# One dense block's expert sums kept in two PSUM banks over all 64 expert pairs, the other four blocks on two banks instead of four

## The chip, the core and the metric

The kernel runs on one core of a Trainium2 chip. The metric is the device time of one execution in microseconds (us), lower is better. Three runs before the change gave 3097.13, 3100.46 and 3105.5 us; the median is 3100.46 us. A core has five engines that run side by side and meet only at semaphores: TensorE (PE in the profile, PEld its weight load), VectorE (DVE), ScalarE (ACT), GpSimd (POOL) and SyncE (SP, which issues DMAs). PE writes only to PSUM, which here is used as eight banks of 128 partitions x 512 float32.

## The reference, cut to what matters

One transformer layer over 1024 tokens of width 1024: a mixer (pooling and windowed attention), then a layer of 16384 one-neuron experts, of which each of 8 heads picks 16 for each token.

```python
u = jnp.take(expert_down, eb, axis=0)
act = jax.nn.gelu(jnp.einsum('td,thkd->thk', hb, u))
wv = gb * act
vv = jnp.take(expert_up, eb, axis=0)
y = jnp.einsum('thk,thkd->td', wv, vv)
x = x + y
return rms_norm(x, g_final)
```

For one token this is the sum over its chosen experts of gate x gelu(h . down) x up. Summed over all 16384 experts with a gate of zero for those not chosen it is the same number, and that is the form the change touches.

## The kernel before, in words

Three stages follow one another: the mixer (and the choice of experts), a table of gates, and `experts`, which starts near 1240 us and ends the kernel. Only `experts` is changed.

The 1024 tokens are 8 blocks of 128. Three blocks (`DB`) are done *by rows*: POOL gathers the chosen experts' rows from HBM by indirect DMA (512 KB for 128 tokens), and DVE multiplies and adds them (L1517 for the down rows, L1529 for the up rows). There are 3 x 256 = 768 such row steps. Up to eight gathers (`RU`) are under way or unread at a time. The other five blocks (`ND`) are done *densely*: PE multiplies them with all 128 tiles of 128 experts. The tiles come in 64 pairs (`NPAIR`), and the loop over pairs `p` drives every engine; each pair also carries 12 of the row steps.

In pair `p`, PE alternates two kinds of work. `down_half(p + 1, q, half)` (L1381 to L1383, 24 matmuls) multiplies a half of the five blocks with a down tile of the *next* pair, into `abank` (two banks). Its two halves done, the semaphore `a_ready` lets ACT apply gelu (L1430), DVE multiply by the gates (`weights`, L1565), ACT make the rounded copy `w_hi` and DVE the rest `w_lo` (`weights_rest`, L1569). `up_product(p, t)` (L1397 to L1399, 12 matmuls in two groups of six) multiplies the weights of block `t` with both up tiles of pair `p`, into two banks of `ybank`, one for each half of the 1024 columns. The order of PE in a pair is written out: down, up 0, down, up 1, down, up 2, down, up 3, up 4. Each operand is split in a rounded high part and a low part, hence three matmuls per product.

After each up product DVE adds its two banks to the running sum `y` in SBUF (`add_y`, L1576, one instruction for each bank). A bank may be written again only when its last content has been added: PE waits on `y_added`. With four banks, product number `n` (over all pairs) waits for the adds of product `n - 2`.

Where DVE meets these adds is fixed by its own program. In pair `p`: `add_y(p - 1, 4)`; 3 row steps; `add_y(p, 0)`; 3 row steps; `weights(p + 1, 0)`; 1 row step; `add_y(p, 1)`; `weights_rest(p + 1, 0)`; 3 row steps; `add_y(p, 2)`; 2 row steps; `weights(p + 1, 1)`; `add_y(p, 3)`; `weights_rest(p + 1, 1)`. POOL's program in pair `p` is: 2 gathers, `down_rest` (L1336), 4 gathers, `up_rest` (L1340), 2 gathers, `down_rest`, 4 gathers, `up_rest`. `down_rest` makes the low part of a down tile and needs ACT's rounded copy of it (`down_high_of`, L1418), which ACT makes after the gelu of the same half pair.

After the loop DVE adds the last product, and the five blocks are normalised (L1498, L1545) and stored.

Of the kernel before, what the change touches and what calls it, by code (L numbers as in the profile page):

```python
# [6 lines left out]
P = 128  # L7
# [22 lines left out]
ND = NBLK - DB  # L30
# [9 lines left out]
F32 = mybir.dt.float32  # L40
# [3 lines left out]
ALU = mybir.AluOpType  # L44
# [1035 lines left out]
NPAIR = NK // 2  # L1080
# [119 lines left out]
def experts(nc, io, scr):  # L1200

    NOP = 8
    with ExitStack() as ctx:
# [3 lines left out]
        def sem(name):  # L1207
            return ctx.enter_context(nc.semaphore(name))
# [11 lines left out]
        tup_hi, tup_lo = sb("tup_hi", [P, 2, 2, D], F32R), sb("tup_lo", [P, 2, 2, D], F32R)  # L1220
        gates = sb("gates", [P, 2, NTC, 2, TC])
        w = sb("w", [P, 2, DT])
        w_hi, w_lo = sb("w_hi", [P, 2, 2, DT], F32R), sb("w_lo", [P, 2, 2, DT], F32R)
        y = sb("y", [P, ND, D])
        h2T = up[:, 0:KD * DT // D].rearrange("p a d -> p (a d)").rearrange("p (k n) -> p k n", k=KD)
        abank = ctx.enter_context(nc.psum_tensor("abank", [P, 2, 512], F32))
        ybank = [ctx.enter_context(nc.psum_tensor(f"ybank{i}", [P, 512], F32)) for i in range(4)]
        acc = ctx.enter_context(nc.psum_tensor("acc", [P, D], F32))
        h2_row = acc

# [21 lines left out]
        w_ready, w_high, w_low = sem("w_ready"), sem("w_high"), sem("w_low")  # L1252
        y_ready = sem("y_ready")
        y_added = sem("y_added")
        y_in = sem("y_in")

        block = ctx.enter_context(nc.Block())
# [111 lines left out]
        @block.tensor  # L1369
        def _(pe):  # L1370
            def down_half(p, q, half, first=False):
                if half == 0:
                    pe.wait_ge(down_low, 2 * p + q + 1)
                    if 2 * p + q:
                        pe.wait_ge(gl_ready, 2 * p + q)
                out, ts = abank[:, half, 0:HT], slice(half * HT, (half + 1) * HT)
                for k in range(KD):
                    if first:
                        pe.wait_ge(h2T_low, k + 1)
                    at = slice(k * P, (k + 1) * P)  # L1380
                    nc.tensor.matmul(out, tdown_hi[:, q, at], h2T_hi[:, k, ts], start=k == 0, stop=False)  # L1381
                    nc.tensor.matmul(out, tdown_hi[:, q, at], h2T_lo[:, k, ts], start=False, stop=False)  # L1382
                    ins = nc.tensor.matmul(out, tdown_lo[:, q, at], h2T_hi[:, k, ts], start=False, stop=k == KD - 1)  # L1383
                if half == 1:
                    ins.then_inc(a_ready, 1)

            def up_product(p, t):
                if t == 0:
                    pe.wait_ge(w_low, 2 * (p + 1))
                    pe.wait_ge(up_low, 2 * (p + 1))  # L1390
                r, n, ts = p % 2, ND * p + t, slice(t * P, (t + 1) * P)
                for i in range(2):
                    if n >= 2:
                        pe.wait_ge(y_added, 2 * (n - 2) + i + 1)
                    out, ds = ybank[n % 2 * 2 + i][:], slice(i * 512, (i + 1) * 512)
                    for q in range(2):
                        nc.tensor.matmul(out, w_hi[:, r, q, ts], tup_hi[:, r, q, ds], start=q == 0, stop=False)  # L1397
                        nc.tensor.matmul(out, w_hi[:, r, q, ts], tup_lo[:, r, q, ds], start=False, stop=False)  # L1398
                        ins = nc.tensor.matmul(out, w_lo[:, r, q, ts], tup_hi[:, r, q, ds], start=False, stop=q == 1)  # L1399
                    ins.then_inc(y_ready, 1)  # L1400

            for q in range(2):
                for half in range(2):
                    down_half(0, q, half, first=q + half == 0)
            for p in range(NPAIR):
                for t in range(ND):
                    if p + 1 < NPAIR and t < 4:
                        down_half(p + 1, t // 2, t % 2)
                    up_product(p, t)

        @block.scalar
        def _(act):
            def down_high_of(p, q):

                act.wait_ge(tdown_in[q], 16 * (p + 1))
                if p:
                    act.wait_ge(a_ready, 2 * (p - 1) + q + 1)
                nc.scalar.activation(tdown_hi[:, q], tdown[:, q], ACT.Copy).then_inc(down_high, 1)  # L1418

            def up_high_of(p, q):  # L1420
                act.wait_ge(tup_in[q], 16 * (p + 1))
                if p >= 2:
                    act.wait_ge(y_ready, 2 * ND * (p - 1))
                nc.scalar.activation(tup_hi[:, p % 2, q], tup[:, q], ACT.Copy).then_inc(up_high, 1)  # L1424

            def expert_gelu(p, q):
                act.wait_ge(a_ready, 2 * p + q + 1)
                if p:
                    act.wait_ge(w_low, 2 * (p - 1) + q + 1)
                nc.scalar.activation(w[:, q].rearrange("p (h n) -> p h n", h=2), abank[:, :, 0:HT],  # L1430
                                     ACT.Gelu_apprx_tanh).then_inc(gl_ready, 1)

            def weights_high(p, q):
                act.wait_ge(w_ready, 2 * p + q + 1)
                if p >= 2:
                    act.wait_ge(y_ready, 2 * ND * (p - 1))
                nc.scalar.activation(w_hi[:, p % 2, q], w[:, q], ACT.Copy).then_inc(w_high, 1)

            def keep_h2(b):
                act.wait_ge(h2_in, 16 * (b + 1))  # L1440
                if b:
                    act.wait_ge(acc_read, b)
                nc.scalar.activation(h2_row[:], h2[:], ACT.Copy).then_inc(h2_kept, 1)

            def root(c, n):
                act.wait_ge(var_ready, c + 1)
                nc.scalar.activation(stat[:, 2, 0:n], stat[:, 1, 0:n], ACT.Sqrt).then_inc(std_ready, 1)

            def row_events(rows):

                for n in rows:
                    kind, b, k = ROWS[n]
                    if kind == "dot" and k == NSEL - 1:
                        act.wait_ge(row_used, n + 1)
                        nc.scalar.activation(act_of[:, b], act_of[:, b], ACT.Gelu_apprx_tanh).then_inc(dots_act, 1)
                    if kind == "up" and k == NSEL - 1:
                        if b + 1 < DB:
                            keep_h2(b + 1)
                        root(b, 1)

            down_high_of(0, 0)
            act.wait_ge(h2T_in, 32)
            for k in range(KD):
                nc.scalar.activation(h2T_hi[:, k], h2T[:, k], ACT.Copy).then_inc(h2T_halved, 1)
            down_high_of(0, 1)
            for q in range(2):
                up_high_of(0, q)
            for q in range(2):
                expert_gelu(0, q)
                down_high_of(1, q)  # L1470
            for q in range(2):
                weights_high(0, q)
            keep_h2(0)
            for p in range(NPAIR):
                a, b = parts(rows_of_pair(p), (5, 5))
                if p + 1 < NPAIR:
                    up_high_of(p + 1, 0)
                row_events(a)
                if p + 1 < NPAIR:
                    expert_gelu(p + 1, 0)  # L1480
                if p + 2 < NPAIR:
                    down_high_of(p + 2, 0)
                if p + 1 < NPAIR:
                    up_high_of(p + 1, 1)
                    weights_high(p + 1, 0)
                row_events(b)
                if p + 1 < NPAIR:
                    expert_gelu(p + 1, 1)
                if p + 2 < NPAIR:
                    down_high_of(p + 2, 1)  # L1490
                if p + 1 < NPAIR:
                    weights_high(p + 1, 1)
            act.wait_ge(normed, DB)
            for t in range(ND):
                act.wait_ge(y_added, 2 * (ND * (NPAIR - 1) + t + 1))
                if t == 0:
                    act.wait_ge(row_used, NROW)
                nc.scalar.activation(up[:, t], y[:, t], ACT.Square, accum_out=stat[:, 0, t:t + 1]).then_inc(ssq_ready, 1)  # L1498
            root(DB, ND)

        @block.vector
        def _(dve):
# [66 lines left out]
                nc.vector.tensor_tensor(w_lo[:, p % 2, q], w[:, q], w_hi[:, p % 2, q].bitcast(F32), ALU.subtract).then_inc(w_low, 1)  # L1569

            def add_y(p, t):
                n = ND * p + t
                for i in range(2):
                    dve.wait_ge(y_ready, 2 * n + i + 1)
                    part = y[:, t, i * 512:(i + 1) * 512]
                    nc.vector.tensor_tensor(part, part, ybank[n % 2 * 2 + i][:], ALU.add).then_inc(y_added, 1)  # L1576

            for k in range(KD):
                dve.wait_ge(h2T_halved, k + 1)
# [7 lines left out]
            for p in range(NPAIR):  # L1587
                more = p + 1 < NPAIR
                a, b, c, d, e = parts(rows_of_pair(p), (3, 2, 1, 3, 1))
                if p:  # L1590
                    add_y(p - 1, ND - 1)
                for n in a:
                    row(n)
                add_y(p, 0)
# [111 lines left out]
```

## Time and profile before

| | us |
|---|---|
| median of three runs | 3100.46 |
| the profiled execution | 3103.28 |
| its span | 3101.5 |
| `experts`, about | 1240 to 3101.5 |
| the 61 pairs from 1321.2 to 3035 | 1713.8 |

| engine | busy over the span | in 1321.2 to 3035 |
|---|---|---|
| PE | 2827.1 us (91%) | 1699.4 us (99%) |
| DVE | 2338.5 us (75%) | 1525.4 us (89%) |
| POOL | 2130.4 us (69%) | 1355.7 us (79%) |
| ACT | 929.9 us (30%) | 416.2 us (24%) |

The second column is the sum over two windows of the trace. A busy PE is one that has a matmul in its pipeline; consecutive matmuls overlap, so the durations of single ones (0.31 and 0.39 us) are longer than the distance between their starts (0.14 and 0.23 us). A row "[0.79 <-DMA up<-in_down,e_idx]" in a timeline says that the engine stood idle for 0.79 us before this instruction and that the landing of that DMA ended it. "x2" behind a row is two like instructions merged into one row, whose duration is then from the start of the first to the end of the second.

### The profile page before, as it was taken

To read this page: it belongs to the slowest core of one execution; us is meant where nothing else is said; L and a number is where in the kernel's file an instruction comes from. 1 tells how busy PE (TensorE), PEld (TensorE's weight loads), DVE (VectorE), ACT (ScalarE), POOL (GpSimd) and SP (SyncE) were. 2 spreads that over 40 slices of the span, in tenths; PEclk is the share of its full clock that TensorE was granted. 3 is DMA by queue.
4 is the path that set the end of the run, shared out by engine and by line. 5 is a ranking of instruction groups with operands and counts; after the bars stand their busy time and mean duration, and the time that the engine had idled before them with its cause. 6 is when DMAs were issued, how large, how long until landed. Compare 5 with 4: busy or idle time off the path is not lost.

```text
span 3101.5 us, 40038 instructions
## 1 busy us (share of the span) xinstructions
PE 2827.1 (91%) x15235; PEld 2473.4 (80%) x15235; DVE 2338.5 (75%) x4356; ACT 929.9 (30%) x1230; POOL 2130.4 (69%) x1553
## 2 busy tenths in 40 slices
PE   7999889998791598699999999999999999999996
PEld 6688777676681487599989998999999989999985
DVE  2322497335399698488898888898898888899888
ACT  4232433222430498222222222222222222222221
POOL 4334576246576697577887877788777877788774
PEclk9899999899895799799999999999999999999998
DMA  4122421022310378988999998989988889998886
GB/s 143 35 68 96 163 69 63 33 68 75 135 56 0 86 225 237 331 323 328 328 327 326 328 330 301 328 327 329 326 328 326 330 300 329 327 330 321 327 318 223
DMA packets 268048, 716.48 MB, mean 231 GB/s; under 512 B 20496, under 2 KB 106256, under 8 KB 267728
## 3 DMA queue, kind: packets, MB, share of 16 engines
q0 software_dynamic: 111152, 404.54, 34.9%
q1 hardware_dynamic: 156704, 309.38, 30.2%
q8 instruction: 121, 1.98, 0.2%
q14 instruction: 71, 0.58, 0.1%
HBM read 657.47 MB, written 56.36 MB: 230 GB/s over the span
## 4 chain that ended last, share of the span: by engine, by line
PE 48%; DVE 4%; POOL 3%; DMA 3%; issue 1%; ACT 1%; DVEq 0%; SPq 0%; ACTq 0%
PE abank L1383 8%; PE abank L1381 8%; PE abank L1382 8%; PE ybank L1397 8%; PE ybank L1398 8%; PE ybank L1399 8%; DVE acc L1529 2%; DMA up<-in_up,e_idx 2%; POOL up L1331 2%; POOL tdown_lo L1336 1%; DVE y L1576 1%; POOL tup_lo L1340 0%; DVE up L1517 0%; DMA up<-in_down,e_idx 0%; DMA e_h<-all_h 0%
## 5 line engine op out<-in xcount | busy, mean ns | idle before, releaser
L1381 PE MATMUL abank<-h2T_hi,tdown_hi 128*128 128x320 f32 x2048 | 634.3, 310 | 38.8 <-DVE h2T_lo L1580 30.8
L1383 PE MATMUL abank<-h2T_hi,tdown_lo 128*128 128x320 f32 x2048 | 634.7, 310 | 0.0
L1382 PE MATMUL abank<-h2T_lo,tdown_hi 128*128 128x320 f32 x2048 | 634.4, 310 | 0.0
L1529 DVE SCALAR_TENSOR_TENSOR acc<-up,e_act,acc 128x1024 f32<-128x1024 f32 x381 | 489.5, 1285 | 87.1 <-DMA up<-in_up,e_idx 70.8
L728 POOL TENSOR_TENSOR m_wlo<-m_raw,m_whi 128x1024 fp32r<-128x1024 f32 x116 | 279.5, 2416 | 381.0 <-ACT m_whi L554 378.7
L1517 DVE CUSTOM_DVE_ANT_0 up<-up,acc 128x1024 f32<-128x1024 f32 x384 | 458.9, 1214 | 104.4 <-DMA up<-in_down,e_idx 94.3
L1397 PE MATMUL ybank<-tup_hi,w_hi 128*128 128x512 f32 x1280 | 504.3, 394 | 18.3 <-DVE y L1576 16.6
L1398 PE MATMUL ybank<-tup_lo,w_hi 128*128 128x512 f32 x1280 | 503.5, 393 | 0.0
L1399 PE MATMUL ybank<-tup_hi,w_lo 128*128 128x512 f32 x1280 | 500.4, 391 | 0.0
L1331 POOL DMA_INDIRECT up<-in_down,e_idx x384 | 406.0, 1057 | 98.2 <-issue 86.3
L1331 POOL DMA_INDIRECT up<-in_up,e_idx x384 | 399.2, 1040 | 103.4 <-issue 88.9
L1336 POOL TENSOR_TENSOR tdown_lo<-tdown,tdown_hi 128x1024 fp32r<-128x1024 f32 x128 | 308.6, 2411 | 204.0 <-ACT tdown_hi L1418 202.5
L1381 PEld LDWEIGHTS abank<-h2T_hi,tdown_hi 128*128 128x128 f32 x2048 | 386.6, 189 | 50.0 <-issue 40.2
L1576 DVE TENSOR_TENSOR y<-y,ybank 128x512 f32<-128x512 f32 x640 | 407.9, 677 | 0.7 <-PE ybank L1399 0.7
L1382 PEld LDWEIGHTS abank<-h2T_lo,tdown_hi 128*128 128x128 f32 x2048 | 386.5, 189 | 9.8
L1383 PEld LDWEIGHTS abank<-h2T_hi,tdown_lo 128*128 128x128 f32 x2048 | 386.2, 189 | 0.0
L1430 ACT ACTIVATE w<-abank 128x640 f32<-128x640 f32 x128 | 90.2, 705 | 904.5 <-PE abank L1383 904.5
L1340 POOL TENSOR_TENSOR tup_lo<-tup,tup_hi 128x1024 fp32r<-128x1024 f32 x128 | 309.4, 2417 | 9.4 <-ACT tup_hi L1424 7.2
L1397 PEld LDWEIGHTS ybank<-tup_hi,w_hi 128*128 128x128 f32 x1280 | 241.7, 189 | 65.8 <-DVE y L1576 19.9
L1399 PEld LDWEIGHTS ybank<-tup_hi,w_lo 128*128 128x128 f32 x1280 | 241.8, 189 | 52.7
L389 PE MATMUL bank<-m_hT,m_whi 128*128 128x512 f32 x656 | 264.3, 403 | 15.1 <-POOL m_wlo L728 12.1
L1398 PEld LDWEIGHTS ybank<-tup_lo,w_hi 128*128 128x128 f32 x1280 | 241.9, 189 | 40.8
(220 smaller groups left out, 4636.0 us busy)
## 6 DMA issues: line engine op xcount, KB each, us to landing
tdown<-in_downT SPq DMA_DIRECT2D x128, 512.0 KB, 6.5
tup<-in_up SPq DMA_DIRECT2D x128, 512.0 KB, 6.5
m_raw<-in_tiles SPq DMA_DIRECT2D x116, 512.0 KB, 3.3
all_table<-t_out SPq DMA_DIRECT2D x10, 4096.0 KB, 16.3
gates<-all_table SPq DMA_DIRECT2D x64, 640.0 KB, 5.0
up<-in_down,e_idx POOLq DMA_INDIRECT x384, 6.5
up<-in_up,e_idx POOLq DMA_INDIRECT x384, 6.7
m_x<-in_x SPq DMA_DIRECT2D x8, 512.0 KB, 5.8
```

The source lines that it names most:

```text
L1331: nc.gpsimd.indirect_dma_start(up[:, n % RU], None, io["up" if kind == "up" else "down"], bass.IndirectOffsetOnAxis(idx[:, b, k:k + 1], 0) ...
L1336: nc.gpsimd.tensor_tensor(tdown_lo[:, q], tdown[:, q], tdown_hi[:, q].bitcast(F32), ALU.subtract).then_inc(down_low, 1)
L1340: nc.gpsimd.tensor_tensor(tup_lo[:, p % 2, q], tup[:, q], tup_hi[:, p % 2, q].bitcast(F32), ALU.subtract).then_inc(up_low, 1)
L1381: nc.tensor.matmul(out, tdown_hi[:, q, at], h2T_hi[:, k, ts], start=k == 0, stop=False)
L1382: nc.tensor.matmul(out, tdown_hi[:, q, at], h2T_lo[:, k, ts], start=False, stop=False)
L1383: ins = nc.tensor.matmul(out, tdown_lo[:, q, at], h2T_hi[:, k, ts], start=False, stop=k == KD - 1)
L1397: nc.tensor.matmul(out, w_hi[:, r, q, ts], tup_hi[:, r, q, ds], start=q == 0, stop=False)
L1398: nc.tensor.matmul(out, w_hi[:, r, q, ts], tup_lo[:, r, q, ds], start=False, stop=False)
L1399: ins = nc.tensor.matmul(out, w_lo[:, r, q, ts], tup_hi[:, r, q, ds], start=False, stop=q == 1)
L1517: nc.vector.tensor_tensor_reduce(out=src, in0=src, in1=h2_row[:], scale=1.0, scalar=0.0, op0=ALU.mult, op1=ALU.add, accum_out=act_of[:, b, ...
L1529: nc.vector.scalar_tensor_tensor(out=acc[:], in0=src, scalar=act_of[:, b, k:k + 1], in1=acc[:], op0=ALU.mult, op1=ALU.add).then_inc(row_us ...
L1576: nc.vector.tensor_tensor(part, part, ybank[n % 2 * 2 + i][:], ALU.add).then_inc(y_added, 1)
```

## The change

`ybank` shrinks from four banks to two. The two banks gained become `ykept`, and the products of the last dense block (`t == 4`) of all 64 pairs accumulate in them: the start flag is set at pair 0 alone and the stop flag at pair 63. DVE adds `ykept` to `y` once, after the loop, so `add_y(p - 1, 4)` is gone from the loop. The products of blocks 0 to 3 share two banks, so that each waits for the adds of the product *just before it* among these four, and block 4 waits for no add. A new semaphore `pair_done` counts the products of block 4 and takes the place of `y_ready` where ACT waits for a whole pair to be done before it overwrites `tup_hi` or `w_hi`.

```diff
-        ybank = [ctx.enter_context(nc.psum_tensor(f"ybank{i}", [P, 512], F32)) for i in range(4)]
+        ybank = [ctx.enter_context(nc.psum_tensor(f"ybank{i}", [P, 512], F32)) for i in range(2)]
+        ykept = [ctx.enter_context(nc.psum_tensor(f"ykept{i}", [P, 512], F32)) for i in range(2)]
...
-                r, n, ts = p % 2, ND * p + t, slice(t * P, (t + 1) * P)
+                r, n, ts = p % 2, (ND - 1) * p + t, slice(t * P, (t + 1) * P)
+                kept = t == ND - 1
                 for i in range(2):
-                    if n >= 2:
-                        pe.wait_ge(y_added, 2 * (n - 2) + i + 1)
-                    out, ds = ybank[n % 2 * 2 + i][:], slice(i * 512, (i + 1) * 512)
+                    if not kept and n >= 1:
+                        pe.wait_ge(y_added, 2 * (n - 1) + i + 1)
+                    out, ds = (ykept if kept else ybank)[i][:], slice(i * 512, (i + 1) * 512)
                     for q in range(2):
-                        nc.tensor.matmul(out, w_hi[:, r, q, ts], tup_hi[:, r, q, ds], start=q == 0, stop=False)
+                        first, last = (p + q == 0, p + 1 == NPAIR and q == 1) if kept else (q == 0, q == 1)
+                        nc.tensor.matmul(out, w_hi[:, r, q, ts], tup_hi[:, r, q, ds], start=first, stop=False)
...
-                    ins.then_inc(y_ready, 1)
+                    ins.then_inc(pair_done if kept else y_ready, 1)
...
-                    act.wait_ge(y_ready, 2 * ND * (p - 1))
+                    act.wait_ge(pair_done, 2 * (p - 1))
...
-                act.wait_ge(y_added, 2 * (ND * (NPAIR - 1) + t + 1))
+                act.wait_ge(y_added, 2 * ((ND - 1) * (NPAIR - 1) + t + 1))
...
-                    dve.wait_ge(y_ready, 2 * n + i + 1)
+                    if kept:
+                        dve.wait_ge(pair_done, 2 * p + i + 1)
+                    else:
+                        dve.wait_ge(y_ready, 2 * n + i + 1)
...
-                if p:
-                    add_y(p - 1, ND - 1)
                 for n in a:
                     row(n)
```

No engine's other instructions move. On DVE at the end of a pair and the start of the next one, before the change (L1565 is `weights`, L1576 an add, L1569 `weights_rest`, L1517 a row step):

```order
L1565 TENSOR_TENSOR w<-w,gates 128x640 [waits gl_ready]
L1576 TENSOR_TENSOR y<-y,ybank0 128x512 [waits y_ready]
L1576 TENSOR_TENSOR y<-y,ybank1 128x512 [waits y_ready]
L1569 TENSOR_TENSOR w_lo<-w,w_hi 128x640 [waits w_high]
L1576 TENSOR_TENSOR y<-y,ybank2 128x512 [waits y_ready]
L1576 TENSOR_TENSOR y<-y,ybank3 128x512 [waits y_ready]
L1517 ISA up,e_act<-up,acc 128x1024 [waits up_in0]
```

and the same place of the changed kernel, whose lines are up to ten higher (L1571, L1586, L1575, L1523):

```order
L1571 TENSOR_TENSOR w<-w,gates 128x640 [waits gl_ready]
L1586 TENSOR_TENSOR y<-y,ybank0 128x512 [waits y_ready]
L1586 TENSOR_TENSOR y<-y,ybank1 128x512 [waits y_ready]
L1575 TENSOR_TENSOR w_lo<-w,w_hi 128x640 [waits w_high]
L1523 ISA up,e_act<-up,acc 128x1024 [waits up_in0]
```

The two adds of block 4 are gone; the first row step of the next pair follows `weights_rest` at once. On PE, at the end of the up product of one block and the start of `down_half` behind it nothing moves; what changes is the bank that each product writes, and so the add it waits for. The first matmul into each bank of the products of blocks 2, 3 and 4 in one pair, before:

```order
L1397 MATMUL ybank0<-tup_hi,w_hi 128x512 [waits y_added]
...
L1397 MATMUL ybank1<-tup_hi,w_hi 128x512 [waits y_added]
...
L1397 MATMUL ybank2<-tup_hi,w_hi 128x512 [waits y_added]
...
L1397 MATMUL ybank3<-tup_hi,w_hi 128x512 [waits y_added]
...
L1397 MATMUL ybank0<-tup_hi,w_hi 128x512 [waits y_added]
...
L1397 MATMUL ybank1<-tup_hi,w_hi 128x512 [waits y_added]
```

and after (L1403 is the line that was L1397):

```order
L1403 MATMUL ybank0<-tup_hi,w_hi 128x512 [waits y_added]
...
L1403 MATMUL ybank1<-tup_hi,w_hi 128x512 [waits y_added]
...
L1403 MATMUL ybank0<-tup_hi,w_hi 128x512 [waits y_added]
...
L1403 MATMUL ybank1<-tup_hi,w_hi 128x512 [waits y_added]
...
L1403 MATMUL ykept0<-tup_hi,w_hi 128x512
...
L1403 MATMUL ykept1<-tup_hi,w_hi 128x512
```

Products 1, 2 and 3 now write the bank that the product just before them wrote, and the one of block 4 waits for nothing on DVE.

## Rows read from the trace of the kernel before

**Rows 1.** Two windows: length; PE, PEld, DVE, ACT, POOL busy; clock; DMA share; GB/s.

```profile
1321.20:2024.70 703.50, 697.17 (x3902) 635.56 (x3901) 624.42 (x832) 171.40 (x205) 555.97 (x399) 1.00 0.89 324
2024.70:3035.00 1010.30, 1002.26 (x5616) 912.75 (x5615) 900.97 (x1149) 244.80 (x294) 799.71 (x576) 1.00 0.90 324
```

**Rows 2.** Waits over the span: who for whom, us, times, longest.

```profile
POOL tdown_lo L1336 <- ACT tdown_hi L1418: 202.5, 68, 23.3
DVE up L1517 <- DMA up<-in_down,e_idx: 94.3, 95, 3.9
DVE acc L1529 <- DMA up<-in_up,e_idx: 70.8, 79, 2.1
PE ybank L1397 <- DVE y L1576: 16.6, 7, 6.2
```

**Rows 3.** Timeline of PE, pair 26: products 0, 2, 3, next 0.

```profile
2024.72 0.39 PE L1397 MATMUL ybank<-tup_hi,w_hi 128*128 128x512 f32 x1
...
2030.84 0.31 PE L1383 MATMUL abank<-h2T_hi,tdown_lo 128*128 128x320 f32 x1
...
2037.24 0.39 PE L1397 MATMUL ybank<-tup_hi,w_hi 128*128 128x512 f32 x1
...
2043.50 0.39 PE L1397 MATMUL ybank<-tup_hi,w_hi 128*128 128x512 f32 x1
...
2052.48 0.39 PE L1397 MATMUL ybank<-tup_hi,w_hi 128*128 128x512 f32 x1
```

**Rows 4.** Timeline of DVE, pair 26, from before add 1 to add 2.

```profile
2033.24 2.77 DVE L1565 TENSOR_TENSOR w<-w,gates 128x640 f32<-128x640 f32 x1
...
2037.07 1.27 DVE L1576 TENSOR_TENSOR y<-y,ybank 128x512 f32<-128x512 f32 x2
...
2041.01 1.22 DVE L1517 CUSTOM_DVE_ANT_0 up<-up,acc 128x1024 f32<-128x1024 f32 x1 [0.79 <-DMA up<-in_down,e_idx]
...
2042.55 1.22 DVE L1517 CUSTOM_DVE_ANT_0 up<-up,acc 128x1024 f32<-128x1024 f32 x1 [0.32 <-DMA up<-in_down,e_idx]
...
2043.70 0.68 DVE L1576 TENSOR_TENSOR y<-y,ybank 128x512 f32<-128x512 f32 x1
```

**Rows 5.** Timelines of ACT and POOL, pair 26, after the second down half.

```profile
2031.18 0.71 ACT L1430 ACTIVATE w<-abank 128x640 f32<-128x640 f32 x1 [8.15 <-PE abank L1383]
...
2032.91 2.41 POOL L1336 TENSOR_TENSOR tdown_lo<-tdown,tdown_hi 128x1024 fp32r<-128x1024 f32 x1 [2.27 <-ACT tdown_hi L1418]
2035.48 1.36 POOL L1331 DMA_INDIRECT up<-in_down,e_idx  x1 [0.16 <-issue]
```

**Rows 6.** Timelines in pair 42: product 3, add 2, product 4.

```profile
2488.42 0.39 PE L1397 MATMUL ybank<-tup_hi,w_hi 128*128 128x512 f32 x1
...
2496.83 1.28 DVE L1576 TENSOR_TENSOR y<-y,ybank 128x512 f32<-128x512 f32 x2
...
2497.57 0.80 PE L1397 MATMUL ybank<-tup_hi,w_hi 128*128 128x512 f32 x1 [6.24 <-DVE y L1576]
```

**Rows 7.** Timelines, pairs 1 and 61: product 3 and add 2.

```profile
1339.97 0.39 PE L1397 MATMUL ybank<-tup_hi,w_hi 128*128 128x512 f32 x1
1340.74 1.28 DVE L1576 TENSOR_TENSOR y<-y,ybank 128x512 f32<-128x512 f32 x2
...
3026.37 0.39 PE L1397 MATMUL ybank<-tup_hi,w_hi 128*128 128x512 f32 x1
...
3026.63 1.28 DVE L1576 TENSOR_TENSOR y<-y,ybank 128x512 f32<-128x512 f32 x2
```

**Rows 8.** PE windows (busy, clock, DMA) after waits of pairs 10, 42.

```profile
1593.40:1603.00 9.60, 9.59 (x52) 1.00 0.87 284
2498.00:2506.00 8.00, 8.00 (x36) 0.74 0.77 236
```

**Rows 9.** Timeline of PE in pair 10: product 4.

```profile
1593.41 0.50 PE L1397 MATMUL ybank<-tup_hi,w_hi 128*128 128x512 f32 x1 [0.69 <-DVE y L1576]
```

**Rows 10.** L1565 over the span: duration ns min/median/max.

```profile
L1565 DVE TENSOR_TENSOR w<-w,gates x128: 815/1342/2765, 1272.3 to 3056.6; 128x640 f32<-128x640 f32 x128
```

More of the change, by code:

```diff
@@ L1254, in experts @@
         y_added = sem("y_added")
+        pair_done = sem("pair_done")
         y_in = sem("y_in")
@@ L1390, in up_product @@
                     pe.wait_ge(up_low, 2 * (p + 1))
-                r, n, ts = p % 2, ND * p + t, slice(t * P, (t + 1) * P)
+                r, n, ts = p % 2, (ND - 1) * p + t, slice(t * P, (t + 1) * P)
+                kept = t == ND - 1
                 for i in range(2):
-                    if n >= 2:
-                        pe.wait_ge(y_added, 2 * (n - 2) + i + 1)
-                    out, ds = ybank[n % 2 * 2 + i][:], slice(i * 512, (i + 1) * 512)
+                    if not kept and n >= 1:
+                        pe.wait_ge(y_added, 2 * (n - 1) + i + 1)
+                    out, ds = (ykept if kept else ybank)[i][:], slice(i * 512, (i + 1) * 512)
                     for q in range(2):
-                        nc.tensor.matmul(out, w_hi[:, r, q, ts], tup_hi[:, r, q, ds], start=q == 0, stop=False)
+                        first, last = (p + q == 0, p + 1 == NPAIR and q == 1) if kept else (q == 0, q == 1)
+                        nc.tensor.matmul(out, w_hi[:, r, q, ts], tup_hi[:, r, q, ds], start=first, stop=False)
                         nc.tensor.matmul(out, w_hi[:, r, q, ts], tup_lo[:, r, q, ds], start=False, stop=False)
-                        ins = nc.tensor.matmul(out, w_lo[:, r, q, ts], tup_hi[:, r, q, ds], start=False, stop=q == 1)
-                    ins.then_inc(y_ready, 1)
+                        ins = nc.tensor.matmul(out, w_lo[:, r, q, ts], tup_hi[:, r, q, ds], start=False, stop=last)
+                    ins.then_inc(pair_done if kept else y_ready, 1)
             for q in range(2):
@@ L1435, in weights_high @@
                 if p >= 2:
-                    act.wait_ge(y_ready, 2 * ND * (p - 1))
+                    act.wait_ge(pair_done, 2 * (p - 1))
                 nc.scalar.activation(w_hi[:, p % 2, q], w[:, q], ACT.Copy).then_inc(w_high, 1)
@@ L1571, in add_y @@
             def add_y(p, t):
-                n = ND * p + t
+                n = (ND - 1) * p + t
+                kept = t == ND - 1
                 for i in range(2):
-                    dve.wait_ge(y_ready, 2 * n + i + 1)
+                    if kept:
+                        dve.wait_ge(pair_done, 2 * p + i + 1)
+                    else:
+                        dve.wait_ge(y_ready, 2 * n + i + 1)
                     part = y[:, t, i * 512:(i + 1) * 512]
-                    nc.vector.tensor_tensor(part, part, ybank[n % 2 * 2 + i][:], ALU.add).then_inc(y_added, 1)
+                    nc.vector.tensor_tensor(part, part, (ykept if kept else ybank)[i][:], ALU.add).then_inc(y_added, 1)
             for k in range(KD):
```

## The prediction

> **What bounds the kernel now.** I read the busy shares by window first. In the steady loop, 1713.8 us for 61 pairs, PE is busy for 1699.4, so it stands idle for 14.4 us in all; DVE is at 89%, POOL at 79%, and the clock at its higher level (2.4 GHz, shown as 1.00) [rows 1]. PE is the bound, and DVE time that is saved is worth something only where PE waits for DVE. The waits of PE on an add come to 16.6 us in 7 places [rows 2]. A pair takes 2052.48 - 2024.72 = 27.76 us [rows 3], and 58 of the 63 pairs keep that time to 0.1 us or so but for pair 21, which is 8.5 us longer.
>
> The question is then how near the adds run behind the products. In pair 26, product 2 starts at 2037.24 [rows 3], and the first add of product 1 starts at 2037.07 and takes 0.68, so ends at 2037.75 [rows 4]. Product 3 starts at 2043.50 [rows 3], the first add of product 2 ends at 2043.70 + 0.68 = 2044.38 [rows 4]. With four banks neither matters. With two, both products would have had to wait.
>
> **Part 1: the two adds of block 4 that go.** 63 pairs x 2 adds, each 0.64 us (two take 1.28 [rows 7]) and paced at about 0.60, are 76 to 81 us of DVE. Nearly all of it is hidden: PE has 14.4 us of idle time to give back at most. I count it at nothing in the steady pairs, since DVE's next step is held by something else: it waits 94.3 + 70.8 = 165.1 us for gathers [rows 2], 2.6 us a pair. 1.2 us sooner at the start of a pair becomes 1.2 us more of that wait at the third row step. At the end of the kernel, where no tile parts are left to make and DVE runs row steps without a pause, one pair of adds (1.2 us) does come off the time.
>
> **Part 2: the bank wait.** What is late next is the add before each product, by how much depends on what sets the add's time. I followed add 2 of pair 26 back. Before it stand two row steps that waited for their gathers, 0.79 and 0.32 us [rows 4]. The gather for the first of them was issued at 2035.48, right behind `tdown_lo`, which started at 2032.91 when ACT's rounded copy came; that came behind the gelu at 2031.18, for which ACT had waited 8.15 us on PE [rows 5]: PE's last matmul of the second down half, at 2030.84 [rows 3]. So the time of add 2 hangs on PE's own work of the same pair, 2044.38 - 2030.84 = 13.54 us behind it, through ACT, POOL and a DMA of about 5.5 us (2041.01 - 2035.48). Neither the removed adds nor a PE that waits at product 2 or 3 changes that distance. A wait at product 3 therefore comes again in every pair and moves the whole pair behind it; it is not a delay that is paid once.
>
> Add 1 hangs on the same event: `weights` at 2033.24 takes 2.77 us instead of 0.815 [rows 4, 10], running beside `tdown_lo` and ending 0.7 us after it (2032.91 + 2.41 [rows 5]; 2036.01), then one row step, then the add. Product 2 would start 2037.75 - 2037.24 + 0.06 = 0.57 us late. The 0.06 is what a release costs: in pair 42 the first add ends at 2496.83 + 0.68 = 2497.51 and the waiting matmul starts at 2497.57 [rows 6]. Product 3 starts late by 2044.38 - 2043.50 + 0.06 = 0.94 us. The two are not added: product 3's start is fixed by add 2, whether product 2 was late or not, so the larger counts.
>
> I took this difference in every pair from 1 to 63. The first is 1340.74 + 0.68 - 1339.97 = 1.45 and pair 61 3026.63 + 0.68 - 3026.37 = 0.94 [rows 7]. Five pairs (10, 32, 42, 59, 63) are apart; over the other 58 the larger of the two differences has a mean of 1.16 (1.17 with the negative one of pair 62 set to nothing), and only that one of the 58 is below zero. Products 0 and 1 are safe in nearly all: 2.8 and 1.0 us of room. The second bank of each product has 0.7 to 0.8 us more room than the first.
>
> 58 x (1.16 + 0.06) = 70.8 us.
>
> The pairs apart: in pair 42 DVE finishes a row block and is 9 us late with add 2. PE got past product 3 at 2488.42 and waited 6.24 us at product 4, until 2497.57 [rows 6]. Now product 3 waits until then, and product 4, one product of 12 matmuls (2.75 us: 12 x 0.23), comes after. So this pair costs one product more, about 2.7 us. Pair 10 is the same with a small wait (0.69, at 1593.41 [rows 9]); for 32 and 59 I take the same: 4 x 2.7 = 10.8. Pair 63 has no down halves, PE waits there in any case and DVE's row block ends later than all products: nothing. Pair 0: product 1 would wait 6 us, but the next pair then waited for the weights anyway; I take 1.
>
> Sum: 70.8 + 10.8 + 1 - 1.2 = 81.4. With a pair of 29.0 us the DMA share of 0.90 [rows 1] falls to about 0.86, and gathers may land a little sooner; I take 0.05 us a pair off, -3. That leaves +78. The profiled execution took 3103.3 against a median of 3100.5, so from the median: 3100.5 + 78.4 = 3179.
>
> **Bounds.** Least: if gathers land so early that DVE no longer waits before add 2, it comes 0.79 + 0.32 = 1.11 us sooner and product 3 has room; what is left is product 2's wait, on which no gather bears. 58 x 0.6 (the median of that difference, 0.55, and the 0.06) = 35, and 10 for the pairs apart: 3145. Most: add 2 later than now by one `weights` (below), 58 x 0.8 = 46 more: 3225.
>
> **ACT's waits** on `pair_done` come true at the same matmul as before (the end of product 4), two pairs back; they cost nothing. The final adds are in the place they had.
>
> **Rivals.**
>
> *Only product 2 waits.* As under the least bound: 3145. For it: DMA is the busiest thing beside PE, and a slower pair relieves it. Against: the wait before add 2 would have to shrink by all of 1.1 us, for 4% less traffic.
>
> *The lock turns round.* `weights` and `tdown_lo` run one after the other today, `tdown_lo` first [rows 4, 5]. With DVE 1.2 us ahead, `weights` may start in the gap between the gelu's end (2031.18 + 0.71 = 2031.89) and 2032.91 [rows 5], and then POOL waits for 0.8 us [rows 10]; the gathers behind it and add 2 come as much later. Time: 3179 + 58 x 0.8 = 3225. The page "SBUF — State Buffer" of the Trainium skill (section "Who interferes with whom") says that a DVE instruction with two SBUF inputs contends with a GpSimd one that reads SBUF, and that issue order decides who blocks. The 2.77 us against 0.815 [rows 4, 10] agree with the first half. Against this rival: the step before `weights` is also held by gathers, so the 1.2 us are mostly gone by then.
>
> *Waits too short to see.* If all of DVE's steps move forward by the 1.2 us saved, add 1 and add 2 end before their products want the banks (0.57 and 0.94 are below 1.2), only the four pairs apart pay, and the time is 3100.5 + 10 - 3 = 3107, inside what counts as no change: a measurement of this kernel can tell 0.3%, 9 us, from none. Against: the waits for gathers named in part 2.
>
> *Faster.* One mechanism: PE's present waits on DVE, 14.4 us in all, go with DVE's load, at the pairs where DVE is late from a finished row block. It decides if the adds there run ahead by more than a product (2.75 us), so that the two-bank rule never binds. Time: 3100.5 - 14.4 - 1.2 = 3085. Against: in pair 42 DVE is 9 us late.
>
> *The clock.* PE now pauses once or twice in each pair. After the wait of 6.24 us of pair 42 the granted clock was 0.74 over 8 us, so for half of that at the lower level (1.2 GHz); after the 0.69 us of pair 10 it was 1.00 over 9.6 us [rows 8, 9]. If a wait of about 1 us cost like the long one, 2 us of work lost each time, the time would be 3179 + 62 x 2 = 3303. The page "TensorE: Matmul & The Clock Gate" of the Trainium skill (section "A second HAM failure mode: psum-queue depth-cycling") speaks for it: a PE that pauses briefly between groups of matmuls while it cycles through PSUM banks can swing between its two clocks. By this trace's short wait it does not.
>
> **Chances.** Forecast 0.63 (its own range 3163 to 3198: 0.95 to 1.5 us a pair), only product 2 waits 0.12, lock 0.11, clock 0.04: slower by over 0.3% together 0.90. Waits too short to see 0.06: same. Faster 0.04. The range takes in the two neighbours up to their bounds, 3142 to 3216.
>
> **What the profile after would show.** DVE's line of adds with 514 instead of 640 instructions. PE idle before the first matmul of product 3 (L1403), released by DVE's add, about 60 times and about 1.2 us each, some 0.6 of it already at product 2; PE's busy share in the loop at 95 or 96%; a pair of 29.0 us; DVE's waits for gathers longer by about 2.4 us a pair (the 1.2 saved and the 1.2 of the longer pair); the granted clock still 1.00. It would be wrong if PE's idle time at L1403 is below 0.3 us a pair, if the distance from the second down half's end to add 2 is not about 13.5 us, or if the clock falls.

## The result, and the profile after

The changed kernel takes 3173.57 us (median of six runs, 3168.19 to 3185.41) against 3100.49 us: a ratio of 1.0238, 95% interval 1.0213 to 1.0262. It is slower by 73 us; 78 us had been forecast. The profiled execution took 3168.92 us with a span of 3167.1, 65.6 us over the span before. Its mean granted clock is 0.957, before it was 0.955.

The windows over the same loop, in the columns of [rows 1]:

```profile
1320.00:2050.00 730.00, 704.38 (x3886) 633.04 (x3885) 604.36 (x783) 172.98 (x205) 551.58 (x400) 1.00 0.86 312
2050.00:3099.00 1049.00, 1013.85 (x5601) 910.75 (x5600) 866.98 (x1073) 246.04 (x294) 795.45 (x574) 1.00 0.86 311
```

PE is busy for 1718.2 of 1779 us, 96.6% where it was 99.2%; the DMA share fell from 0.90 to 0.86, and the clock stayed at 1.00. The waits, in the columns of [rows 2]:

```profile
POOL tdown_lo L1340 <- ACT tdown_hi L1424: 274.8, 100, 23.1
DVE up L1523 <- DMA up<-in_down,e_idx: 161.7, 111, 4.1
DVE acc L1535 <- DMA up<-in_up,e_idx: 115.5, 91, 4.0
PE ybank L1403 <- DVE y L1586: 66.0, 87, 8.3
```

PE's waits on an add went from 7 with 16.6 us to 87 with 66.0 us. DVE's waits for gathers rose by 112 us, 1.8 us a pair. This is DVE's row of the costliest groups (add instructions, busy time, mean, idle before it):

```profile
L1586 DVE TENSOR_TENSOR y<-y,ybank 128x512 f32<-128x512 f32 x512 | 327.8, 678 | 11.4 <-PE ybank L1405 11.3
```

With the two adds of `ykept` at the end there are 514 instead of 640. The 126 adds took some 79 us of DVE with them (the row before has 407.9 us for 640), and the time rose.

Over the pairs 1 to 61, product 3 waits in 60 and product 2 in 37. One pair shows both waits. PE in pair 22 (the starts of product 0, of the last matmul of the second down half, of products 1, 2, 3 with its second matmul, and of the next product 0), which answers to [rows 3]:

```profile
1934.37 0.39 PE L1403 MATMUL ybank<-tup_hi,w_hi 128*128 128x512 f32 x1
...
1940.48 0.31 PE L1387 MATMUL abank<-h2T_hi,tdown_lo 128*128 128x320 f32 x1
1940.63 0.39 PE L1403 MATMUL ybank<-tup_hi,w_hi 128*128 128x512 f32 x1
...
1947.45 0.50 PE L1403 MATMUL ybank<-tup_hi,w_hi 128*128 128x512 f32 x1 [0.40 <-DVE y L1586]
...
1954.07 0.50 PE L1403 MATMUL ybank<-tup_hi,w_hi 128*128 128x512 f32 x1
1954.41 0.40 PE L1404 MATMUL ybank<-tup_lo,w_hi 128*128 128x512 f32 x1
...
1963.15 0.39 PE L1403 MATMUL ybank<-tup_hi,w_hi 128*128 128x512 f32 x1
```

and DVE in it, which answers to [rows 4]:

```profile
1943.64 2.01 DVE L1571 TENSOR_TENSOR w<-w,gates 128x640 f32<-128x640 f32 x1
...
1946.72 1.27 DVE L1586 TENSOR_TENSOR y<-y,ybank 128x512 f32<-128x512 f32 x2
...
1950.93 1.22 DVE L1523 CUSTOM_DVE_ANT_0 up<-up,acc 128x1024 f32<-128x1024 f32 x1 [1.06 <-DMA up<-in_down,e_idx]
...
1953.34 1.28 DVE L1586 TENSOR_TENSOR y<-y,ybank 128x512 f32<-128x512 f32 x2
```

The first add of product 1 ends at 1946.72 + 0.68 = 1947.40 and product 2 starts at 1947.45; the first add of product 2 ends at 1954.02 and product 3 starts at 1954.07. The steps between products are 6.82 and 6.62 us where they were 6.26, and the pair takes 28.78 us. The timelines of ACT and POOL, against [rows 5]:

```profile
1940.83 0.71 ACT L1436 ACTIVATE w<-abank 128x640 f32<-128x640 f32 x1 [8.65 <-PE abank L1387]
...
1942.56 2.41 POOL L1340 TENSOR_TENSOR tdown_lo<-tdown,tdown_hi 128x1024 fp32r<-128x1024 f32 x1 [3.25 <-ACT tdown_hi L1424]
1945.12 1.36 POOL L1335 DMA_INDIRECT up<-in_down,e_idx  x1
```

From PE's last matmul of the second down half to the end of the first add of product 2 it is 1954.02 - 1940.48 = 13.54 us, as in pair 26 before (that the second decimal agrees is chance; the medians are below). The chain that ended last tells the same: PE had 48% of the span in it and now has 22%, DMA 14% (3% before), DVE 10% (4%), POOL 7% (3%).

### The profile page after: what moved, and what is told of

Same layout as the page of the kernel before. It is cut to its first block, busy times and chain, and to the rows that moved or that the text cites. A ratio compares the mean times of both kernels' runs of the same rounds, so it can differ in the third digit from the quotient of the medians.

```text
span 3167.1 us, 39912 instructions
## 1 busy us (share of the span) xinstructions
PE 2850.9 (90%) x15235; PEld 2473.3 (78%) x15235; DVE 2285.4 (72%) x4230; ACT 934.0 (29%) x1230; POOL 2126.1 (67%) x1553
## 4 chain that ended last, share of the span: by engine, by line
PE 22%; DMA 14%; DVE 10%; POOL 7%; issue 5%; ACT 2%; DVEq 0%; SPq 0%; ACTq 0%
DMA up<-in_up,e_idx 7%; DMA up<-in_down,e_idx 6%; POOL tdown_lo L1340 4%; DVE acc L1535 4%; PE abank L1387 4%; PE abank L1385 4%; PE abank L1386 4%; PE ybank L1403 3%; PE ybank L1404 3%; PE ybank L1405 3%; POOL up L1335 3%; DVE up L1523 2%; ACT tdown_hi L1424 2%; DVE y L1586 2%; DVE w L1571 1%
## 5 line engine op out<-in xcount | busy, mean ns | idle before, releaser
L1523 DVE CUSTOM_DVE_ANT_0 up<-up,acc 128x1024 f32<-128x1024 f32 x384 | 459.5, 1216 | 169.6 <-DMA up<-in_down,e_idx 161.7
L1403 PE MATMUL ybank<-tup_hi,w_hi 128*128 128x512 f32 x1024 | 414.3, 405 | 68.2 <-DVE y L1586 66.0
L1335 POOL DMA_INDIRECT up<-in_down,e_idx x384 | 393.2, 1024 | 97.7 <-issue 83.0
L1404 PE MATMUL ybank<-tup_lo,w_hi 128*128 128x512 f32 x1024 | 403.7, 394 | 0.0
L1405 PE MATMUL ybank<-tup_hi,w_lo 128*128 128x512 f32 x1024 | 401.7, 392 | 0.0
L1586 DVE TENSOR_TENSOR y<-y,ybank 128x512 f32<-128x512 f32 x512 | 327.8, 678 | 11.4 <-PE ybank L1405 11.3
L1403 PEld LDWEIGHTS ybank<-tup_hi,w_hi 128*128 128x128 f32 x1024 | 193.8, 189 | 128.3 <-DVE y L1586 92.7
L391 PE MATMUL bank<-m_hT,m_wlo 128*128 128x512 f32 x656 | 257.9, 393 | 0.0
L390 PE MATMUL bank<-m_hlo,m_whi 128*128 128x512 f32 x656 | 257.2, 392 | 0.0
```

What stands on the lines that cost most here:

```text
L1335: nc.gpsimd.indirect_dma_start(up[:, n % RU], None, io["up" if kind == "up" else "down"], bass.IndirectOffsetOnAxis(idx[:, b, k:k + 1], 0) ...
L1523: nc.vector.tensor_tensor_reduce(out=src, in0=src, in1=h2_row[:], scale=1.0, scalar=0.0, op0=ALU.mult, op1=ALU.add, accum_out=act_of[:, b, ...
L1586: nc.vector.tensor_tensor(part, part, (ykept if kept else ybank)[i][:], ALU.add).then_inc(y_added, 1)
```

## The experiments

Below, *distance* is the time from the modelled end of that last down matmul (about 0.3 us after its start) to the end of the first add of product 2, as the median over the pairs 1 to 61: 13.60 us before, 13.36 us in the changed kernel. *Pair* is the median time of a pair: 27.76 and 28.93. All are edits of the changed kernel unless said otherwise. Each ratio is against runs of the kernel before made beside that experiment, whose medians are 3099.05, 3100.0 or 3103.2 us, so it can differ a little from the quotient with 3100.49.

**Both adds early.** DVE's order alone.

```diff
-                a, b, c, d, e = parts(rows_of_pair(p), (3, 2, 1, 3, 1))
+                a, b, c, d, e = parts(rows_of_pair(p), (3, 3, 1, 1, 4))
...
+                add_y(p, 1)
                 if more:
                     weights(p + 1, 0)
                 for n in c:
                     row(n)
-                add_y(p, 1)
```

> The changed kernel with DVE's order alone altered: the add of block 1 goes ahead of `weights(p+1, 0)` and one row step, the add of block 2 ahead of the two row steps that wait for their gathers (it stands behind one row step and not three). If the loss is the bank wait and nothing else, the first add of product 1 ends near 10 us into the pair and that of product 2 near 16.2, both before the 12.5 and 18.8 at which PE wants the banks: PE's wait for DVE falls under 15 us, a pair is back at 27.8 us, and the time is 3100 us (3090 to 3108). If the loss lay in the accumulation over 64 pairs itself, in the clock, or in DVE and POOL blocking each other in another order, the time stays near 3170.

Measured: 3103.86 us, ratio 1.0009 (1.0001 to 1.0018). Pair 27.76. Nothing but the place of two adds was altered, and 70 of the 73 us are back; accumulation over 64 pairs costs nothing that shows in a steady pair. PE's waits on adds did not fall under the 15 us expected; this is what is left of them (who waited for whom, us, times, longest):

```profile
PE ybank L1403 <- DVE y L1586: 18.1, 5, 6.9
```

**Add 1 early alone** (the second half of that edit, with the shares left as they were).

> The changed kernel with only the add of block 1 moved ahead of `weights(p+1, 0)` and one row step. If the waits of one pair are not added, because product 3 starts when add 2 is done whether product 2 was late or not, then product 2's wait of 0.6 us goes and product 3's grows to the full 1.2: 3173 us (3167 to 3180). If they are added, 0.6 us x 61 = 35 us come back: 3138.

Measured: 3198.4 us, ratio 1.031 (1.0292 to 1.0329). Product 2 no longer waits (6.26 us from product 1), and nothing came back, so the waits do not add, as expected. But it is 25 us slower still, which neither side had. The distance grew to 13.78 us and the pair to 29.33. PE waits once a pair (97.0 us in 65 places).

The 0.4 us more of distance come at row step 9 (steps are numbered from 0 within a pair). Step 8 starts where it did, 10.0 us behind the down half. Step 9 starts at 11.94 and not 11.49, though its gather is issued at 5.99 us in both kernels: it lands 5.89 us after its issue and not 5.48 (all medians). Why it lands later is not settled.

**Add 2 early alone** (the shares of the first edit, add 1 where it was).

> The changed kernel with only the add of block 2 moved, to stand before the two row steps that wait for their gathers. Product 3's wait goes and product 2's stays at 0.6 us: a pair of 28.4 us, 3173 - 61 x 0.6 = 3137 us (3128 to 3147). If the two waits had one cause apart from the place of the add (a slower DVE, the clock), the time stays near 3173.

Measured: 3140.89 us, ratio 1.0139 (1.0125 to 1.0154). Pair 28.45, which is 0.69 over 27.76, with all of it at product 2 (6.86 us from product 1, so a wait of 0.60); product 3 starts 6.37 us after it. As expected, but for the last 0.1 us: product 3 itself does not wait, and 6.37 is 0.11 over 6.26. That is what PE loses behind a wait, beside the wait (below, under the sum). PE's waits on adds are 44.5 us in 63 places.

**Two gathers early.** POOL's order alone: row steps 8 and 9 are gathered ahead of `tdown_lo`.

```diff
-                a, b, c, d = parts(rows_of_pair(p), (2, 3, 2, 3))
+                a, b, c, d = parts(rows_of_pair(p), (2, 4, 4, 2))
```

> The changed kernel with POOL's order alone altered: two gathers of the last part of a pair (row steps 8 and 9) go ahead of the `tdown_lo` that waits for ACT, two stay behind it. My account says that add 2 hangs on that chain: PE's second down half, gelu, rounded copy, `tdown_lo`, gather. Then row steps 8 and 9 find their rows there, add 2 comes about 1 us sooner, product 3's wait beyond product 2's goes: 3140 us (3130 to 3155). If add 2 is late for another reason (DVE's own load, the DMA engines' traffic), the time stays within 8 us of 3173, or rises because `tdown_lo` starts later.

Measured: 3133.09 us, ratio 1.0108 (1.0092 to 1.0125). The distance fell to 10.33 us. No instruction of DVE or PE was touched, and 40 us are back: the adds were late through the gathers behind `tdown_lo`.

The time is in the range expected, but by another mix of pairs than the one expected, and so by luck. Add 2 came 3.0 us sooner, not 1. Product 2's wait did not stay in every pair: of the pairs 1 to 61, 42 take 27.8 us and wait for no add. In 45 pairs `weights` had run ahead of `tdown_lo`, and add 1 was in time. Another 18 take over 29 us, most of them 30.2. In 17 of these 18 (not in pair 42, where DVE finishes a row block), and in no other pair, the first `w_lo` of the pair takes over 1.5 us. Pair 26, DVE and then POOL:

```profile
2049.10 3.45 DVE L1575 TENSOR_TENSOR w_lo<-w,w_hi 128x640 fp32r<-128x640 f32 x1
...
2055.89 1.27 DVE L1586 TENSOR_TENSOR y<-y,ybank 128x512 f32<-128x512 f32 x2
```

```profile
2049.45 2.40 POOL L1344 TENSOR_TENSOR tup_lo<-tup,tup_hi 128x1024 fp32r<-128x1024 f32 x1
```

`w_lo`, 0.82 us at the median, takes 3.45 us and ends 0.7 us after `tup_lo`: the same picture as `weights` beside `tdown_lo` in [rows 4, 5]. This pair has the longest `w_lo`; in the others `tup_lo` starts some 0.2 us ahead of `w_lo`, which then takes 2.9 us.

**One gather early** (shares 2, 4, 3, 3), to test that reading.

> The changed kernel with one gather (row step 8) moved ahead of `tdown_lo`, three behind it, where an earlier experiment moved two. There, the POOL subtraction `tup_lo` came 6.9 us behind PE's second down half, just before DVE's `w_lo` at about 7.1, and 26 `w_lo` took over 1.5 us and not 0.8 (3 in the changed kernel); its pairs took 27.8 or 30.2 us. With three gathers behind it `tup_lo` starts near 8.2, after `w_lo`. If DVE and POOL blocked each other there, the 30.2 us pairs go and no more than some five `w_lo` are long; row step 9 still starts about 1.5 us sooner than in the changed kernel, so that product 3 waits little beyond product 2: 3133 us (3120 to 3148). If the 30.2 us pairs have another cause, they stay.

Measured: 3139.19 us, ratio 1.0109 (1.0092 to 1.0126). Pair 28.45: the pairs of 27.8 and 30.2 us are gone but for single ones. `tup_lo` came 8.8 us behind the down half. Product 2's 0.6 us is what is left. The time was hit. `w_lo` took over 1.5 us 15 times, not 26 and not the expected five, but 13 of the 15 are the second `w_lo` of a pair, beside a `tdown_lo`, and these pairs take 28.4 or 28.8 us but for the pairs 0 and 21, which are long in every kernel. At the place that made the slow pairs, the first `w_lo` beside `tup_lo`, no pair from 1 to 61 has a long one. That the two blocked each other there is borne out; that the blocking moved to the second `w_lo` was not expected.

**The bank rule alone.** Block 4 gets its two banks but starts afresh in each pair, and DVE adds it in each pair.

```diff
-                        first, last = (p + q == 0, p + 1 == NPAIR and q == 1) if kept else (q == 0, q == 1)
+                        first, last = q == 0, q == 1
...
+                if p:
+                    add_y(p - 1, ND - 1)
```

(and a semaphore of its own for these adds, on which the next product of block 4 waits.)

> The bank rule without the removed adds: blocks 0 to 3 share two banks, block 4 has its own two, but its products start afresh in each pair and DVE adds them in each pair, as in the kernel before. If the 126 adds are worth nothing in the steady loop, as I counted them, the time is that of the changed kernel, plus 1 to 2 us at the end: 3175 us (3168 to 3182). If DVE's relief had hidden part of the loss, up to 1.2 us a pair, the time is up to 3245.

Measured: 3182.54 us, ratio 1.026 (1.0244 to 1.0275). Pair 28.99, distance 13.44. All of the loss is there without the removed adds. The time lies 0.5 us above the range expected. Beside 1.0238 (1.0213 to 1.0262) of the changed kernel it is 9 us more, but the intervals overlap; the median pair accounts for 0.06 x 61 = 4 us of them.

**The removed adds alone.** The kernel before with four banks; 63 of the 64 sums of block 4 are made and never added.

> The removed adds without the bank rule: the kernel before with its four banks, in which the products of block 4 are made in every pair but added only after the last one (so the sums of block 4 lack 63 of 64 pairs). By my account 1.2 us comes off the end and a few us at the places where DVE is late from a finished row block: 3096 us (3088 to 3100.5). If PE's present waits on DVE all go with the load: 3086. If DVE had been a bound in the steady loop, 27.8 us a pair would fall, and the time with it by tens of us.

Measured: 3098.64 us, ratio 0.9995 (0.9985 to 1.0005). Pair 27.76. 126 adds of DVE are worth nothing that can be measured. In the trace the idle time of DVE before the third row step of a pair grew from 1.19 to 2.11 us (means over the pairs 1 to 61), which is where the prediction said the 1.2 us would go.

**The kernel before, reordered** (four banks, all adds, the order of DVE of the first experiment).

> The kernel before (four banks, all adds) with the order of DVE that the first experiment has: add 1 ahead of `weights(p+1, 0)`, add 2 ahead of the last four row steps. With four banks PE waits for the adds only at the finished row blocks, so the order should be worth little: 3098 us (3092 to 3102). Beside the first experiment it tells what two kept banks are worth once their wait is gone: by my account the 1.2 us at the end and a few us at the row blocks.

Measured: 3094.0 us, ratio 0.998 (0.997 to 0.9991). It is the fastest of all, and beats both kernels.

```profile
PE ybank L1397 <- DVE y L1576: 3.3, 3, 2.1
```

Against the first experiment, with 18.1 us of waits on adds, this is what four banks give where DVE is late, in pair 0 (6.9 of the 18.1 us) and at the finished row blocks: 10 us in the medians, 15 us in the waits. The trace of this kernel is of its fastest execution (3088.46 us), so the 15 says too much. The two kept banks lose to the two spare ones even when no steady pair waits. I had expected the opposite sign.

**Add 2 late.** One more row step ahead of it (the shares are 3, 3, 1, 4, 1).

> The changed kernel with the add of block 2 one row step later (behind rows 7 to 10 of a pair, not 7 to 9). In the changed kernel the add's first half ends 13.36 us behind PE's second down half and a pair takes 28.93; a row step is 1.2 to 1.3 us. If product 3's wait is the whole cause, the distance grows to 14.6 and the pair by the same 1.25 us, one for one: 3173.6 + 61 x 1.25 = 3250 us (3238 to 3262). If part of the delay is caught up elsewhere (DMA relief, other waits), the time rises by less than 60 us.

Measured: 3354.36 us, ratio 1.0797 (1.0773 to 1.082), 181 us over the changed kernel (173 by the two ratios). The expectation of 76 failed, and on the side that I had not named. The distance grew by 2.0 us, to 15.35, and the pair by 3.42, to 32.35. Of the 2.0, 0.57 is row step 9, which starts at 12.06 us behind the down half and not at 11.49, as in the second experiment and as little settled; the rest is the row step added and its wait. The wait of pair 24, and windows over the pairs 24 and 25, the 9.5 us up to the wait's end and the 9.3 us from there on (length, PE busy, clock, DMA share, GB/s):

```profile
2080.76 0.50 PE L1403 MATMUL ybank<-tup_hi,w_hi 128*128 128x512 f32 x1 [3.15 <-DVE y L1586]
```

```profile
2058.67:2125.24 66.57, 60.52 (x314) 0.92 0.77 282
2071.20:2080.70 9.50, 6.42 (x38) 1.00 0.92 329
2080.70:2090.00 9.30, 9.24 (x39) 0.82 0.90 327
```

With waits of some 3 us the clock goes to its lower level (1.2 GHz) for a part of the work: 0.82 in the 9.3 us after this one. The mean granted clock of the execution is 0.934 against 0.957. In the pairs 1 to 61 the trace's record of the clock has 44 stretches at the lower level, 178 us in all, where the changed kernel has 3 and 17 us.

The two parts can be told apart. The distance grew by 1.84 us at the mean, 61 x 1.84 = 112 of the 183 us that these 61 pairs took longer. The other 71 are the clock: in 43 pairs it was low around the start of product 3, and from there to product 4 it took 4.44 us where it was 2.85, 43 x 1.59 = 68. The other 18 pairs waited nearly as long with the clock at its higher level, and there pair time less distance is 15.57 us, the number of the other kernels below.

## Why the prediction was right

*What bounds the kernel.* PE did, as read from the windows, and time saved on DVE was worth nothing: the removed adds alone gave 0.9995 (0.9985 to 1.0005). Of PE's 14.4 us of idle time none came back that can be measured.

*The chain behind add 2.* It was right in all its links, and it is shown, not only argued: moving the add back by its place in DVE's order took the wait at product 3 away, and so did, in 42 of 61 pairs, the place of two gathers in POOL's order, each without the other. With the end of the down half as the starting point, pair time and distance differ by the same number in the three kernels whose pairs wait at product 3: 28.93 - 13.36 = 15.57, 29.33 - 13.78 = 15.55, 28.99 - 13.44 = 15.55. To these come the 18 pairs of the last experiment with 15.57. This difference is PE's own work from product 3 to the next down half; what was forecast is that the distance does not shrink when PE gets later, and it did not, but for 0.2 us. That is the "comes again in every pair" of the prediction. For the kernel before this sum would give 13.60 + 15.56 = 29.16; it took 27.76, since its four banks did not ask for the add.

*The sum.* The 61 pairs from 1 to 61 took 1784.7 us against 1714.2: +70.5. The pairs 10, 32, 42 and 59 gave +4.27, +1.72, +2.44 and +0.02, together 8.5 (forecast 10.8), and pair 21, which I had among the steady ones, -1.4. The other 56 gave +1.13 us each at the mean, 63.5 together (+1.17 at the median; forecast 1.22, less 0.05). The end from pair 62 on is 1.2 us shorter, as forecast. Pair 0 is 1.2 us shorter where I had +1, and the stage began 2.5 us sooner in this execution, which is no effect of the change. 70.5 - 1.2 - 1.2 - 2.5 = 65.6, as the spans have it. Pair 62, which the prediction counts among those that keep 27.76 us, takes 24.2 us in both kernels.

*Two terms of it were too small, and they cancel.* That the steady pair came out so close is in part luck. In means over the 56 pairs, the steps are:

| | forecast | measured |
|---|---|---|
| add 2 ends after product 3 wants to start | 1.16 | 1.18 |
| from the end of the add to the start of the product | 0.06 | 0.07 |
| product 3 takes longer behind a wait | 0 | 0.10 |
| the distance is shorter | -0.05 | -0.21 |
| together | 1.17 | 1.14 |

The prediction had no term for the third. Behind a wait the second matmul starts 0.34 us after the first (1954.07 and 1954.41, above) and not 0.23, and product 4 starts 2.85 us after product 3 and not 2.745. For the fourth it named DMA relief and put it too low. The gathers of row steps 8 and 9 landed 5.60 and 5.48 us after their issue, 5.76 and 5.69 before (medians), while the DMA share fell from 0.90 to 0.86. That is in line with relief; no run changes the traffic alone, so the cause is not shown. DVE's waits for gathers grew by 1.8 us a pair, not by the 2.4 forecast.

*The rivals.* "Only product 2 waits" did not come by itself; the third experiment made it, and gave the 28.45 us pair it said. "Waits too short to see" and "Faster" are answered by the removed adds alone: most of DVE's 1.2 us went into its wait at the third row step, and 0.9985 to 1.0005 leaves no room for 3085 us. In the changed kernel the first adds of products 1 and 2 ended only 0.05 and 0.24 us sooner behind the down half.

"The lock turns round": the event came in a good third of the pairs. In 24 of the pairs 1 to 61 (1 before) `weights` of the first half ran ahead of `tdown_lo`, in about 0.8 us. It ended 2.0 us behind the down half, when `tdown_lo` had its start at 1.77 in the profile. The price was small: `tdown_lo` ended at 4.28 us at the median of these pairs, 4.18 in the others, 4.86 at the latest, and not 0.8 us later each time. And the event has a gain that the rival had not named: these 24 are the very pairs in which product 2 does not wait. The blocking is dear for another pair of instructions, as the two gather experiments show.

"The clock" did not come for waits of 0.6 to 1.2 us, and did for waits of 3 us. The 3 low stretches of the changed kernel lie in the pairs 10, 21 and 42; with add 1 early alone, where product 3 waits about 1.5 us, there are 7, 34 us in all. I had given this rival 0.04 on a wait of 0.69 us against one of 6.24; the short one was the nearer row, and it decided rightly here. The Trainium skill says in "TensorE: Matmul & The Clock Gate", section "A second HAM failure mode: psum-queue depth-cycling", that brief pauses between groups of matmuls make the clock swing. The changed kernel does not show it (3 stretches); with add 2 late, at pauses of some 3 us, the clock does swing (44 stretches).

## What to carry to other kernels

A PSUM bank count is a promise on how late its reader may be; before banks are given away, subtract in the trace each writer's start from the reader's end for the *new* distance in banks, pair by pair. Then follow the reader back: if its time hangs on the bound engine's own work of the same iteration, the wait is paid in every iteration, and work taken from the reader's engine does not buy it back. The cheapest cure here was the place of the reader in its engine's program, ahead of steps that wait for a DMA.

## What the runs showed that I had not expected

- With a wait of PE by some 3 us in each pair the clock was low around 43 of 61 products 3 (0.82 in the 9.3 us behind one of them); with waits of 0.6 to 1.2 us it stayed up. The price of a wait is not linear: 2.0 us more of distance cost 3.4 us a pair.
- A DVE subtraction of two SBUF operands (`w_lo`) took 3.45 us instead of 0.81 when POOL's `tup_lo` of 2.40 us started 0.35 us after it in the profile. The page "SBUF — State Buffer" of the Trainium skill, section "Who interferes with whom", has such a DVE instruction contend with a GpSimd one that reads SBUF; the trace agrees: `w_lo` took 2.64 us longer, about all of the POOL instruction's time, and 2.9 us in the commoner case in which `tup_lo` started first.
- With nothing but two adds moved, the kernel before went to 3094.0 us, and the one with two kept banks to 3103.9: spare banks are worth more here than 126 adds.
